# Routing and first expert of a mixture layer: expert 0 fixed as the first pass, its weights requested from the closing products on, a router held still

## The chip, the cores and the metric

One NeuronCore of a Trainium2 chip. The metric is the device time of one execution in microseconds (us), the median of three runs. One more execution was taken with the hardware profiler; all rows below come from it. PE is the matrix engine, PEld its weight load, DVE the vector engine, ACT the scalar engine, POOL GpSimd, SP the engine whose queue issues most DMAs.

## The reference

One step of a decoder of two layers for 288 tokens (256 of a prompt, 8 sequences of 4), all in float32, model width 1024. Each layer adds `W_out(sum_b sigmoid(x_n W_gate_b) * (branch_b W_branch_b))` to x, over three branches (retention, mLSTM, RWKV). Then layer 0 adds a dense SwiGLU, and layer 1 a mixture of eight experts with hidden width 1408:

```
logits = h @ router                  # h = RMSNorm(x), 288 x 8
top_v, top_i = lax.top_k(logits, 2)
probs = softmax(top_v)
y = y + combine[..., e:e+1] * ((silu(h @ wg[e]) * (h @ wu[e])) @ wd[e])    # e = 0..7
```

A final RMSNorm gives y. The experts' weights are 17.3 MB each, in float32.

## The kernel before

x, its norm xn and all weights lie with the feature on the partition, tokens along the row. Each engine's program is written out by hand and runs in order; semaphores tie them together. SP streams the weights as slabs. For the layer's branch part there is a ring of four slots (RING), of 1024 KB each; `load` waits until PE has freed the slot (slot_fr) and issues one DMA.

**Closing products** (`closing`, lines 1114 to 1141). The last eight of 24 units, 16 to 23, run in a loop of two rounds of four: PE makes the four gate products from slabs of 768 KB (L1079), waits for y_rw, and makes the four branch products (L1086), each of which frees its slab. Then eight output products from four slabs (L1139) read `mixed`; DVE adds them to X (L2074, x_mix). y_rw is written by DVE at L2039 (rw_y), in the arena, the area that also holds the later expert slabs. The norm's squares are summed on PE (L675, nm_ms), ACT takes the root, DVE the reciprocal, and then xn in eight steps (L1684).

**Routing** (`route` in PE's and DVE's program). PE makes the logits with xn as the stationary operand and the router moving: 3 tiles of 128 tokens by 8 products, 8 columns wide (L1148). It transposes xn into six half tiles (L1155), which ACT (L1607) and DVE (L2157) copy to xt. DVE picks the top two (to L2100, rt_sel). PE counts, with a triangle and a matrix of ones, how many tokens ahead chose each expert, and how many in all: 9 products (L1161, L1164, rt_pos). DVE ranks all eight experts by their counts (L2118 to L2126), writes the plan (plan_ok) and goes on to each token's place (to L2151, rt_q). `pick_tokens` turns places into a 0/1 matrix for the first pass (L2183, L2187, in_ok).

**Expert passes** (`experts`). There are eight passes, one an expert. Pass p takes the expert of rank ORDER[p] and has the fixed column count PASSES[p] = WIDTHS[ORDER[p]]: 128, 64, 96, 76, 88, 80, 64, 64. If an expert has more tokens than its width, extra passes of 64 follow, counted at run time. A pass gathers its tokens with products of xt and the 0/1 matrix (L1177 by `gather`), makes 11 gate and 11 up products from 11 slabs (L1177 again, two halves of 64 rows), and the down products in blocks of 32 tokens from six slabs (L1252). The pass after adds the result to the 288 tokens (`scatter`, L1202). The gather for pass p + 1 stands between gate/up and down of pass p. In the first pass, after f = 1, PE spreads each token's choices over the partitions (`broadcast_choices`, L1171).

**Expert slabs.** ETURNS = 17 slabs hold one expert: 0 to 3 in the ring's slots, 4 to 16 in the arena. SP waits for plan_ok, reads the expert's number, and issues all 17 (L645); for later passes each waits until PE has used the same slab of the pass before (e_used). Each slab has its own semaphore.

Every float32 product appears in the profile as two MATMUL and two LDWEIGHTS records.

## Time and profile before

| what | value |
|---|---|
| median of 3 runs | 1855.35 us (1854.37 to 1857.85) |
| the profiled execution's own time | 1862.14 us |
| its span, first to last instruction | 1860.3 us |
| mean granted clock of PE | 0.956 |
| busy: PE, PEld, DVE, ACT, POOL | 1746.0, 1378.5, 598.5, 289.4, 24.6 us |
| read from and written to memory | 275.48 MB, 10.89 MB |

Busy is summed over the whole span, and matmuls are pipelined, so 94% for PE is no measure of how near a stage is to its limit. The layer with the experts takes the last third; its stages are: closing products to 1400, norm and routing to 1439, passes to 1838, the final norm to the end.

### The profile page before, as it was taken

The page shows a single profiled execution, that of the slowest core. Times are in us where ns is not written, and L with a number is a line of the kernel's source. Part 1 is how long each engine was busy: PE and PEld are TensorE (multiplying, and loading weights), DVE is VectorE, ACT ScalarE, POOL GpSimd, SP SyncE. Part 2 cuts the span into 40 slices and gives each one's busy share as a digit, 9 for nine tenths or more (in the row PEclk, how much of TensorE's full clock was granted, in tenths as well). Part 3 has the DMA queues.
Part 4 walks back from the last instruction along what each step waited for, and adds up shares of the span by engine and source line. Part 5 has one row for each costly group of instructions (what it writes and reads, how often), then busy time and mean ns, then how long its engine had stood idle before and what let it go on. Part 6 is the DMA issues. An engine that isn't in the chain of part 4 may idle for free.

```text
span 1860.3 us, 39410 instructions
## 1 busy us (share of the span) xinstructions
PE 1746.0 (94%) x17757; PEld 1378.5 (74%) x17757; DVE 598.5 (32%) x1341; ACT 289.4 (16%) x631; POOL 24.6 (1%) x44
## 2 busy tenths in 40 slices
PE   6999999999899999999999999999997989999887
PEld 4778776788677777776677776787676978778675
DVE  3022617662511000003123526862515222212123
ACT  1321102312101000001321112221111000000001
POOL 0000000000000000000000000000000000000000
PEclk9998989999899999999998999998997999999998
DMA  7211413220253334334221412221323999889880
GB/s 287 91 68 68 158 57 126 86 75 22 58 181 113 129 109 162 121 127 197 71 88 46 177 66 97 102 59 39 101 101 147 422 385 356 331 336 366 312 345 28
DMA packets 58743, 288.80 MB, mean 155 GB/s; under 512 B 21528, under 2 KB 21976, under 8 KB 31832
## 3 DMA queue, kind: packets, MB, share of 16 engines
q1 hardware_dynamic: 39800, 266.34, 38.3%
q0 software_dynamic: 2272, 15.86, 2.2%
q10 hardware_dynamic: 16512, 4.19, 1.1%
q8 instruction: 135, 2.21, 0.5%
q14 instruction: 24, 0.20, 0.0%
HBM read 275.48 MB, written 10.89 MB: 154 GB/s over the span
## 4 chain that ended last, share of the span: by engine, by line
PE 88%; DVE 7%; issue 3%; ACT 1%; ACTq 1%; DMA 0%; DVEq 0%; SPq 0%
PE ps L1177 13%; PE ps L708 13%; PE ps L1291 9%; PE ps L1079 9%; PE ps L1252 6%; PE ps L702 5%; PE ps L1086 5%; PE ps L1300 5%; PE ps L1139 3%; PE ps L951 3%; PE ps L1202 1%; PE ps L675 1%; PE ps L806 1%; PE ps L853 1%; PE ps L781 1%
## 5 line engine op out<-in xcount | busy, mean ns | idle before, releaser
L708 PE MATMUL ps<-xn,ring 128*128 128x288 f32 x960 | 267.2, 439 | 6.5 <-DVE xn L1684 6.5
L708 PEld LDWEIGHTS ps<-xn,ring 128*128 128x128 f32 x960 | 194.9, 206 | 66.8 <-issue 10.2
L1079 PE MATMUL ps<-xn,ring 128*128 128x288 f32 x768 | 207.6, 420 | 0.0
L1079 PEld LDWEIGHTS ps<-xn,ring 128*128 128x128 f32 x768 | 146.6, 195 | 45.2 <-issue 4.6
L1291 PE MATMUL ps<-xn,ring 128*128 128x288 f32 x704 | 172.8, 409 | 3.2 <-DVE xn L1684 3.2
L1291 PEld LDWEIGHTS ps<-xn,ring 128*128 128x128 f32 x704 | 134.8, 192 | 41.1 <-issue 3.6
L1177 PE MATMUL ps<-y_ml,arena 128*64 128x64 f32 (+5 forms) x3584 | 136.5, 238 | 15.1 <-issue 14.9
L1177 PEld LDWEIGHTS ps<-y_ml,arena 128*64 128x64 f32 x3584 | 132.9, 139 | 20.3 <-issue 20.3
L1252 PE MATMUL ps<-arena,mixed 128*32 128x256 f32 x1936 | 108.8, 383 | 1.9 <-issue 1.9
L1252 PEld LDWEIGHTS ps<-arena,mixed 128*32 128x32 f32 x1936 | 62.0, 111 | 47.4 <-issue 6.3
L702 PE MATMUL ps<-ring,xn 128*128 128x256 f32 (+1 forms) x384 | 91.8, 399 | 0.0
L1300 PE MATMUL ps<-arena,ring 128*128 128x288 f32 x352 | 85.7, 406 | 0.0
L1177 PEld LDWEIGHTS ps<-y_ml,ring 128*64 128x64 f32 x2048 | 75.7, 137 | 12.5 <-issue 12.5
L1177 PE MATMUL ps<-y_ml,ring 128*64 128x64 f32 (+5 forms) x2048 | 79.1, 237 | 6.0 <-issue 5.1
L702 PEld LDWEIGHTS ps<-ring,xn 128*128 128x128 f32 (+1 forms) x384 | 64.7, 172 | 24.6 <-issue 6.6
L1300 PEld LDWEIGHTS ps<-arena,ring 128*128 128x128 f32 x352 | 66.9, 190 | 18.5
L2224 DVE TENSOR_TENSOR mixed<-ps,mixed 128x64 f32<-128x64 f32 (+5 forms) x88 | 21.4, 244 | 164.7 <-PE ps L1177 164.6
L1139 PE MATMUL ps<-mixed,ring 128*128 128x288 f32 x256 | 62.6, 407 | 2.5 <-DVE mixed L2066 2.5
L2274 DVE TENSOR_TENSOR arena<-ps,arena 128x288 f32<-128x288 f32 x22 | 10.1, 458 | 160.3 <-PE ps L1291 160.3
L1139 PEld LDWEIGHTS ps<-mixed,ring 128*128 128x128 f32 x256 | 48.5, 190 | 16.6 <-DVE mixed L2066 3.4
L1589 ACT ACTIVATE mixed<-ps 128x64 f32<-128x64 f32 (+5 forms) x88 | 21.1, 240 | 224.0 <-PE ps L1177 224.0
L1692 DVE RECIPROCAL arena<-arena 128x288 f32<-128x288 f32 x24 | 44.3, 1910 | 17.1 <-ACT arena L1430 17.1
(414 smaller groups left out, 1909.2 us busy)
## 6 DMA issues: line engine op xcount, KB each, us to landing
arena<-in_egu SPq DMA_DIRECT2D x56, 1024.0 KB, 7.2
...
```

The source lines that it names most:

```text
L702: last = mm(bank[0:m, 0:256], xn[:, k, c0:c0 + m], ring[:, s, 256 * k:256 * k + 256], start=(k == 0), stop=(k == KT - 1))
L708: last = mm(bank[:, 0:T], ring[:, s, w0:w0 + P], xn[:, k, :], start=(k == 0), stop=(k == KT - 1))
L951: last = mm(ps[half(q), out, CH * (u - 8 * g):CH * (u - 8 * g) + CH], left[half(q), u, :], right(q, u), start=True, stop=True)
L1079: last = mm(ps[:, bank, 0:T], ring[:, s, P * k:P * k + P], xn[:, k, :], start=(k == 0), stop=(k == KT - 1))
L1086: last = mm(ps[:, bank, 0:T], ring[:, s, P * (KT + k):P * (KT + k) + P], y[:, k, :], start=(k == 0), stop=(k == 3))
L1139: last = mm(ps[:, 6 + d % 2, 0:T], ring[:, s, w0:w0 + P], mixed[:, k, :], start=(k == 0), stop=(k == KT - 1))
L1177: last = mm(out(r), stationary(r), moving, start=start, stop=stop, skip_group_check=True)
L1252: last = mm(ps[TB * c:TB * c + TB, 6 + b // 2, 256 * (b % 2):256 * (b % 2) + 256], ehid[:, f, TB * b:TB * b + TB], slab_[:, w0:w0 + 256], ...
L1291: last = mm(ps[:, 2 * (f % 3) + w, 0:T], ring[:, s, w0:w0 + P], xn[:, k, :], start=(k == 0), stop=(k == KT - 1))
L1300: last = mm(ps[:, 6 + d % 2, 0:T], ring[:, s, P * f:P * f + P], hid[:, f, :], start=(f == 0), stop=(f == FT - 1))
L1692: last = dve.reciprocal(sq[:, j, :], sq[:, j, :])
L2224: TT(ehid[:, f, 0:n], ps[:, 2 * (f % 2) + 1, 0:n], esil[:, f % 3, 0:n], MUL).then_inc(e_hid.sem, 1)
```

## The change

- Expert 0 has rank 0 and is always the first pass, with 96 columns (its `tie` constant puts it above all counts). The other seven are ranked by count; their widths are 128, 96, 88, 80, 72, 64, 64. In order of the passes: 96, 72, 128, 80, 96, 88, 64, 64.
- SP's loop over the unit slabs has one round less. In layer 1 SP then waits for y_rw and the RWKV state stores, issues the plan constants and slabs 8 to 15 of expert 0, then the last four unit slabs and the output slabs, then slabs 0 to 3 as the ring's slots come free, and after the norm's sum (nm_ms) slabs 4 to 7 and 16. From pass 1 on it issues as before.
- The logits come from eight products with the router stationary and 288 columns moving, into four column groups of one bank; DVE copies the bank, and three products with the `fold` matrix add the groups and turn the result.
- Counting takes four products instead of nine.
- Expert 0's tokens are picked straight after the counts (three picks, `own`); ranking, plan and places follow. The transposes of the choices move behind f = 1 of the first pass, the broadcast behind f = 3, and `extra_passes` with them.
- ACT copies five of the six half tiles of xt and both halves of the first gathered tile. Two memsets move from DVE to POOL, behind the last x_mix.

```
-WIDTHS = (128, 96, 88, 80, 76, 64, 64, 64)
-ORDER = (0, 6, 1, 4, 2, 3, 5, 7)
+WIDTHS = (96, 128, 96, 88, 80, 72, 64, 64)
+ORDER = (0, 5, 1, 4, 2, 3, 6, 7)
...
+               ("experts", NE), ("fold", NE), ("steps", OVERS), ("extras", MAXEXTRA)):
...
+    put("tie", NE - 1 - np.arange(NE) + NE * 2 * T * (np.arange(NE) == 0))
...
+    put("fold", r[:, None] % TB == np.arange(NE)[None, :])
...
-                with sp.Fori(0, len(UNITS) // 4) as j:
+                rounds = len(UNITS) // 4 - 1
+                with sp.Fori(0, rounds) as j:
                     inner = turns.loop(j, 4)
                     for k in range(4):
                         slab = a["mix"][l, bass.ds(j * 4 + (len(EARLY) + k), 1), :, 0:12 * P]
                         load(inner, slab.rearrange("a p n -> p (a n)"), 12 * P)
-                turns.after(len(UNITS) // 4, 4)
+                turns.after(rounds, 4)
+
+                def first_expert(slabs):
+                    for k in slabs:
+                        src = a["egu"][k] if k < FT else a["edown"][k - FT, :, 0:D * len(DOWN[k - FT])]
+                        sp.dma_start(eslab(k), src).then_inc(e_ld[k].sem, 16)
+
+                if l > 0:
+                    sp.wait_ge(*rw_y(l))
+                    sp.wait_ge(st_rw.sem, 32 * (l + 1))
+                    sp.wait_ge(st_rws.sem, 32 * (l + 1))
+                    sp.dma_start(pcon, a["pcon"]).then_inc(ld_con.sem, 16)
+                    first_expert(range(FREE, ETURNS - 1))
+                for k in range(4):
+                    load(turns, a["mix"][l, len(EARLY) + 4 * rounds + k, :, 0:12 * P], 12 * P)
                 for k in range(4):
                     load(turns, a["mix"][l, len(EARLY) + len(UNITS) + k], SLOT)
...
-                sp.wait_ge(*rw_y(l))
-                sp.dma_start(pcon, a["pcon"]).then_inc(ld_con.sem, 16)
+                for _ in range(RING):
+                    s, n = turns.take()
+                    sp.wait_ge(slot_fr[s].sem, n)
+                    first_expert([s])
+                sp.wait_ge(*nm_ms(2 * l + 1))
+                first_expert([*range(RING, FREE), ETURNS - 1])
                 sp.wait_ge(*plan_ok(0))
-                for p in range(FIXED):
-                    expert(p, p == 0, sp.value_load(plan[0:1, p:p + 1], min_val=0, max_val=NE - 1))
+                for p in range(1, FIXED):
+                    expert(p, sp.value_load(plan[0:1, p:p + 1], min_val=0, max_val=NE - 1))
                 sp.wait_ge(*extra_ok(0))
                 npass = sp.value_load(plan[0:1, PLAN_N - 1:PLAN_N], min_val=1, max_val=1 + MAXEXTRA)
                 with sp.Fori(0, npass) as i:
-                    e = sp.value_load(plan[0:1, bass.ds(i + FIXED, 1)], min_val=0, max_val=NE - 1)
-                    expert(i + FIXED, False, e)
...
+                for k in range(KT):
+                    pe.wait_ge(*nm_xn(3, k + 1))
+                    c = TB * (k % 4)
+                    w0 = LW["router"] + NE * k
+                    last = mm(ps[c:c + NE, 6, 0:T], lw[:, w0:w0 + NE], xn[:, k, :], start=(k < 4), stop=(k >= 4))
+                last.then_inc(rt_part.sem, 1)
+
+                def token_tiles(first, end):
+                    for n in range(first, end):
+                        c0, m = TOK[n // 2]
+                        for k in range(4):
+                            last = pe.transpose(ps[0:m, n, P * k:P * k + P], xn[:, 4 * (n % 2) + k, c0:c0 + m],
+                                                C("ident", P))
+                        last.then_inc(xt_p.sem, 1)
+
+                token_tiles(0, 2)
+                pe.wait_ge(ld_con.sem, 64)
+                pe.wait_ge(*rt_lp(0))
                 for i, (c0, m) in enumerate(TOK):
-                    for k in range(KT):
-                        pe.wait_ge(*nm_xn(3, k + 1))
-                        last = mm(ps[0:m, 6, NE * i:NE * i + NE], xn[:, k, c0:c0 + m],
-                                  lw[:, LW["router"] + NE * k:LW["router"] + NE * k + NE],
-                                  start=(k == 0), stop=(k == KT - 1))
+                    last = mm(ps[0:m, 7, NE * i:NE * i + NE], gate[:, 0, c0:c0 + m], PCON("fold", NE), start=True,
+                              stop=True)
                 last.then_inc(rt_lg.sem, 1)
-                for n in range(6):
-                    c0, m = TOK[n // 2]
-                    for k in range(4):
-                        last = pe.transpose(ps[0:m, n, P * k:P * k + P], xn[:, 4 * (n % 2) + k, c0:c0 + m], C("ident", P))
-                    last.then_inc(xt_p.sem, 1)
-                pe.wait_ge(ld_con.sem, 64)
+                token_tiles(2, 6)
                 pe.wait_ge(*rt_sel(0))
-                for i in range(3):
-                    for k in range(i + 1):
-                        mm(ps[:, 7, NE * i:NE * i + NE], PCON("tri", P) if k == i else C("ones", P), gt[:, k, :],
-                           start=(k == 0), stop=(k == i))
-                for k in range(3):
-                    last = mm(ps[:, 7, 32:32 + NE], C("ones", P), gt[:, k, :], start=(k == 0), stop=(k == 2))
+                mm(ps[:, 7, 64:88], PCON("tri", P), gt, start=True, stop=False, skip_group_check=True)
+                for n in range(3):
+                    last = mm(ps[:, 7, 72 + NE * n:96], C("ones", P), gt[:, 0:3 - n, :], start=False, stop=(n == 2),
+                              skip_group_check=True)
                 last.then_inc(rt_pos.sem, 1)
+
+            def choices():
+
+                pe.wait_ge(*rt_q(0))
+                for i, (c0, m) in enumerate(TOK):
+                    last = pe.transpose(ps[0:4, 6, c0:c0 + m], q[0:m, :, i], C("ident", m, m))
+                last.then_inc(rt_ct.sem, 1)
...
                         if first:
-                            broadcast_choices()
+                            choices()
                         else:
                             scatter(p - 1, blocks, 0)
+                    if f == 3 and first:
+                        broadcast_choices()
                     if f == 3 and not first:
                         scatter(p - 1, blocks, 1)
...
-                pe.wait_ge(xt_a.sem, 3)
-                pe.wait_ge(xt_d.sem, 3)
+                pe.wait_ge(xt_a.sem, 5)
+                pe.wait_ge(xt_d.sem, 1)
                 gather(0, PASSES[0])
-                pe.wait_ge(*rt_q(0))
-                for i, (c0, m) in enumerate(TOK):
-                    last = pe.transpose(ps[0:4, 6, c0:c0 + m], q[0:m, :, i], C("ident", m, m))
-                last.then_inc(rt_ct.sem, 1)
...
-                    if f == 1 and first:
+                    if f == 3 and first:
                         for v, bank in ((0, 7), (2, 5)):
                             act.wait_ge(rt_bc.sem, v + 1)
                             A(chosen[:, v, :], ps[:, bank, 0:T], ACT.Copy).then_inc(rt_cha.sem, 1)
...
-                act.wait_ge(*rt_e(0))
-                A(ex, ex, ACT.Exp).then_inc(rt_ex.sem, 1)
-                for n in (0, 2, 4):
+                for n in range(5):
+                    if n == 4:
+                        act.wait_ge(*rt_e(0))
+                        A(ex, ex, ACT.Exp).then_inc(rt_ex.sem, 1)
+                        act.wait_ge(*rt_sel(0))
                     act.wait_ge(xt_p.sem, n + 1)
                     m = TOK[n // 2][1]
-                    if n == 4:
-                        act.wait_ge(*rt_sel(0))
-                    A(xt[0:m, n // 2, 0:512], ps[0:m, n, :], ACT.Copy).then_inc(xt_a.sem, 1)
+                    h = 512 * (n % 2)
+                    A(xt[0:m, n // 2, h:h + 512], ps[0:m, n, :], ACT.Copy).then_inc(xt_a.sem, 1)
                 gathered(0, PASSES[0])
+                act.wait_ge(ga_p.sem, 2)
+                A(xg[:, 4:8, 0:PASSES[0]], ps[:, 5, :].rearrange("p (k n) -> p k n", k=4)[:, :, 0:PASSES[0]], ACT.Copy)\
+                    .then_inc(ga_d.sem, 1)
...
-                dve.memset(yg, 0.0)
                 link(dve.memset(lg, 0.0))
-                dve.memset(xt[:, 2, :], 0.0)
+                dve.wait_ge(*rt_part(0))
+                dve.tensor_copy(gate[:, 0, :], ps[:, 6, 0:T]).then_inc(rt_lp.sem, 1)
                 dve.wait_ge(*rt_lg(0))
-                dve.tensor_copy(lg[:, 0:2, :], ps[:, 6, 0:16].rearrange("p (i e) -> p i e", i=2))
-                link(dve.tensor_copy(lg[0:TS, 2, :], ps[0:TS, 6, 16:24]))
+                dve.tensor_copy(lg[:, 0:2, :], ps[:, 7, 0:16].rearrange("p (i e) -> p i e", i=2))
+                link(dve.tensor_copy(lg[0:TS, 2, :], ps[0:TS, 7, 16:24]))
...
+                dve.wait_ge(*rt_zero(0))
                 dve.sem_inc(rt_sel.sem, 1)
+                dve.wait_ge(xt_p.sem, 6)
+                dve.tensor_copy(xt[0:TS, 2, 512:D], ps[0:TS, 5, :]).then_inc(xt_d.sem, 1)
+
+                dve.wait_ge(*rt_pos(0))
+                dve.tensor_copy(cnt, ps[:, 7, 88:96])
+                link(dve.tensor_copy(pos, ps[:, 7, 64:88].rearrange("p (i e) -> p i e", i=3)))
+                link(STT(own, pos[:, :, 0], 1.0, gt[:, :, 0], ADD, MUL))
+                for i in range(3):
+                    last = TSC(pick_in[:, i, 0:PASSES[0]], PCON("iota", PASSES[0]), own[:, i:i + 1], None, ALU.is_equal)
+                last.then_inc(in_ok.sem, 1)
...
-                dve.wait_ge(*rt_pos(0))
-                link(dve.tensor_copy(cnt, ps[:, 7, 32:32 + NE]))
-                dve.tensor_copy(pos, ps[:, 7, 0:24].rearrange("p (i e) -> p i e", i=3))
...
-                pick_tokens(0, PASSES[0])
-                for n in (1, 3, 5):
-                    dve.wait_ge(xt_p.sem, n + 1)
-                    m = TOK[n // 2][1]
-                    dve.tensor_copy(xt[0:m, n // 2, 512:D], ps[0:m, n, :]).then_inc(xt_d.sem, 1)
...
-                dve.wait_ge(*rt_ct(0))
-                dve.tensor_copy(gate_rows[0:4, 0, :], ps[0:4, 6, 0:T]).then_inc(rt_cr.sem, 1)
-                next_places(0)
...
-                    if f == 1:
+                    if f == 1 and not first:
+                        scattered(p - 1, 0)
+                    if f == 2:
                         if first:
-                            for v, bank in ((1, 4), (3, 6)):
-                                dve.wait_ge(rt_bc.sem, v + 1)
-                                dve.tensor_copy(chosen[:, v, :], ps[:, bank, 0:T]).then_inc(rt_chd.sem, 1)
-                        else:
-                            scattered(p - 1, 0)
-                    if f == 2:
+                            dve.wait_ge(*rt_ct(0))
+                            dve.tensor_copy(gate_rows[0:4, 0, :], ps[0:4, 6, 0:T]).then_inc(rt_cr.sem, 1)
+                            next_places(0)
                         pick_tokens(p + 1, after)
                         next_places(p + 1)
+                    if f == 3 and first:
+                        extra_passes()
+                        for v, bank in ((1, 4), (3, 6)):
+                            dve.wait_ge(rt_bc.sem, v + 1)
+                            dve.tensor_copy(chosen[:, v, :], ps[:, bank, 0:T]).then_inc(rt_chd.sem, 1)
...
-                gathered(0, PASSES[0])
-                extra_passes()
...
+            pool.wait_ge(*x_mix(DEPTH - 1, 8))
+            pool.memset(yg, 0.0)
+            pool.memset(xt[:, 2, :], 0.0).then_inc(rt_zero.sem, 1)
...
```

## Rows read from the trace of the kernel before

**Rows 1.** Windows, pass by pass: start:end length, busy PE PEld DVE ACT POOL, clock, DMA, GB/s
```profile
1439.14:1501.93 62.79, 62.79 (x1161) 54.03 (x1161) 12.19 (x40) 4.26 (x14) 0.00 (x0) 1.00 1.01 422
1501.93:1549.90 47.97, 40.36 (x1045) 33.95 (x1041) 10.75 (x34) 3.55 (x13) 0.00 (x0) 1.00 0.91 346
1549.90:1603.58 53.68, 50.82 (x1100) 42.40 (x1096) 11.42 (x35) 3.78 (x13) 0.00 (x0) 1.00 0.92 354
1603.58:1654.40 50.82, 46.43 (x1113) 37.97 (x1112) 11.72 (x36) 3.64 (x13) 0.00 (x0) 1.00 0.88 340
1654.40:1703.39 48.99, 48.47 (x1114) 41.09 (x1112) 11.78 (x36) 3.73 (x13) 0.00 (x0) 1.00 0.94 360
1703.39:1757.98 54.59, 48.16 (x1117) 38.68 (x1113) 11.64 (x36) 3.60 (x13) 0.00 (x0) 0.97 0.84 321
1757.98:1802.69 44.71, 39.51 (x1029) 33.53 (x1025) 10.30 (x34) 4.04 (x14) 0.00 (x0) 0.96 0.97 371
```

**Rows 2.** PE timeline in two passes, and the instruction queue between 1500 and 1550 us
```profile
1455.45 24.62 PE L1177 MATMUL ps<-y_ml,arena 128*64 128x128 f32 x448
...
1482.80 19.20 PE L1252 MATMUL ps<-arena,mixed 128*32 128x256 f32 x352
...
1722.57 4.64 PE L1177 MATMUL ps<-y_ml,arena 128*64 128x80 f32 x127 [1.65 <-issue]
1728.86 4.64 PE L1177 MATMUL ps<-y_ml,arena 128*64 128x80 f32 x127 [1.65 <-issue]
...
q8 instruction: 9, 0.15, 1.1%
```

**Rows 3.** Routing: two rows of the timeline, then the chain of waits
```profile
1406.52 3.52 DVE L1684 SCALAR_TENSOR_TENSOR xn<-X,vec,rstd 128x288 f32<-128x288 f32 x8
...
1417.54 0.18 DVE L2100 TENSOR_TENSOR arena<-arena 128x24 f32<-128x24 f32 x1
...
1407.10 7.96 PE ps L1148 x48
1415.06 3.98 PE ps L1155 x24
1419.04 1.24 PE ps L1161 x12
...
1420.99 0.18 DVE arena L2118
...
1427.77 0.69 DVE mixed L2183 x3
...
1429.37 1.79 DVE con L2157 x3
...
1431.25 7.06 PE ps L1177 x96
```

**Rows 4.** Timeline of the closing products, SP, DVE and PE
```profile
1310.42 57.48 SPq L601 DMA_DIRECT2D ring<-in_mix  x9
...
1329.61 1.36 DVE L2039 TENSOR_TENSOR arena<-arena 128x1152 f32<-128x1152 f32 x1
...
1344.09 15.68 PE L1079 MATMUL ps<-xn,ring 128*128 128x288 f32 x64
```

**Rows 5.** Landing times of L645 (1420:1470) and L601 (1300:1400); one window; SP's issues
```profile
DMA to landing us min/median/max: 4.8/21.8/27.7
...
DMA to landing us min/median/max: 4.1/5.7/7.9
...
1420.00:1430.00 10.00, 0.95 (x9) 0.86 (x8) 7.88 (x41) 0.00 (x0) 0.00 (x0) 0.72 0.50 187
...
1423.96 2.16 SPq L645 DMA_DIRECT2D ring<-in_egu  x4
```

**Rows 6.** PE's busy time and granted clock in two stretches after a pause
```profile
1315.00:1322.00 7.00, 6.29 (x13) 0.51 0.55 130
...
1431.00:1434.00 3.00, 2.75 (x26) 0.50 1.03 434
```

36 lines of the change are left out of this document (18 added, 18 removed).

## The prediction

> **What bounds the kernel now.** I read the windows by stage first, because the engine shares are averages over stages. From 1439.14 us on, eight passes over eight experts follow each other, 62.79 us for the first, 44 to 55 us for the next six [rows 1], and one more of two blocks, which the change leaves as it is. The matrix engine (PE) is busy in most of each window, but the DMA share stands beside it at 0.84 to 1.01, so two limits compete there. The gap list settles which. In the 80-column pass PE runs 127 matmul records, pauses 1.65 us, runs 127 records, pauses again [rows 2]. A slab holds 64 records of this work (704 over 11 slabs), so two slabs would be 128, and these pauses do not sit on slab borders. 127 matmuls with their weight loads are 254 instructions, and the instruction queue brings packets one every 50/9 = 5.6 us [rows 2]. I read the pauses as waits for instructions that arrive slowly beside full data queues. The expert weights are ahead of PE: the first slab is requested at 1423.96 [rows 5] and wanted at 1439.14, and one slab takes 2.5 us to move where PE works 3.5 on it (64 records of 0.055). So the passes are set by PE work or by about 6 us per 127 records, whichever is longer.
>
> Ahead of the passes lies the routing, a chain of small steps from 1407.10 to 1439.14 in which PE mostly waits or runs at half clock [rows 3]. Ahead of that are the closing products, where PE has no pause: from 1344.09 it takes the second four gate slabs right behind the first four's branch products [rows 4].
>
> **Part 1: expert 0 is loaded during the closing products.** No wait for expert weights is removed by that, since PE does not wait for them now. What counts is what the new transfers stand in front of. SP issues everything on one queue. Now the last four unit slabs are requested as their slots come free (the nine issues from 1310.42 on [rows 4]). After the change SP first waits for y_rw, which DVE finishes at 1329.61 + 1.36 = 1330.97 [rows 4], then issues the plan constants and slabs 8 to 15, eight of 1024 KB, and only then unit slab 20. The waits for the state stores are over by then. The queue serves in order: the slab loads issued between 1420 and 1470 needed 21.8 us to land in the median, against 5.7 for the unit and output slabs with a nearly free queue [rows 5], with 422 GB/s moved [rows 1]. Start of transfer: 1.87 MB were moved between 1420 and 1430 (187 GB/s) [rows 5], 4.4 us at 422 GB/s, so the first byte flowed at 1425.6, some 1.6 us after the first issue at 1423.96, which is what plan_ok releases [rows 5]. Hence: 1331.0 + 1.6 + 0.4 (the plan constants, some 150 KB) + 8 x 1.049 MB at 422 GB/s (8 x 2.49 = 19.9) = 1352.9, then 0.786 MB of unit slab 20 (1.9) and its landing (0.6, what the shortest time of 4.1 us [rows 5] leaves after 1.6 and 1.9): 1355.4. PE wants the slab at about 1344.2. It stands still for 11.2 us. The next three slabs land 1.9 us apart, faster than the 3.9 us per slab that PE needs (15.68/4 [rows 4]), so nothing is added there. After such a pause the granted clock is at 0.5 (1.2 of 2.4 GHz) and stays there for a while after work resumes: 0.51 over the 7 us from 1315 and 0.50 over the 3 us from 1431 [rows 6]. Half of 3 to 6.5 us is lost: 1.5 to 3.2, I take 2. **Part 1: +13.2 us** (9.5 if the queue starts sooner and the clock holds, 14.5 above).
>
> The remaining nine slabs cost nothing: four go as the output slabs are freed, five (4.7 MB, 11 us) from the norm's sum on, and the first is wanted 20 us later. That cover is the routing; if it shrank under 11 us slab 4 would be late first.
>
> **Part 2: routing.** Times here are on the old clock, without part 1's shift. xn comes in eight steps of 0.44 until 1410.04 [rows 3]. The old router ran 48 records of 8 columns after that, until 1415.06. The new one keeps the router still and moves 288 columns in eight products, in four column groups, and only the last follows xn: 1.0 us at half clock, 1411.0. The copy to SBUF (0.5, as one step of xn over the same 288 columns) lies beside eight transposes (3.98/24 x 8 = 1.3), to 1412.4; three folding products (6 records like the router's, 0.166 each) to 1413.4. That is 1.7 us earlier than 1415.06. The selection is unchanged, 1415.06 to 1417.72 [rows 3], so 1416.1. The POOL memsets that take the place of DVE's run since x_mix, long done. Old: counting waits for the transposes until 1419.04, and DVE has its 18 records at 1420.99. New: 8 records (0.10 each [rows 3], or 0.16 at half clock), 1417.1. Then DVE: cnt, pos, own at 0.2 each, three picks of 96 columns (0.69 x 96/128 = 0.5), gather may start at 1418.4. Old start: 1431.25, because the whole ranking (1420.99 to 1427.77), six picks and three copies (1.79) lay before it [rows 3]. The copies go to ACT, five at 0.6 and one table load, over by 1417.3. The ranking moves behind in_ok: plan at about 1422, choices at 1427. It delays SP's plan_ok, but SP first needs e_used at 1427 anyway; PE's choices come after two slabs, at 1430. The gather is 96 records with 96 instead of 128 columns: 7.06 x 3/4 = 5.3, evacuation by ACT 0.7 (0.83 now, 1438.31 to 1439.14): PE starts the first pass at 1424.4 where it started at 1439.14, 14.7 earlier. The three transposes of the choices move from before into the first pass (+0.5). The added DVE work at f = 2 and 3 (about 2.6 and 3 us) stays within the slab it has in hand. **Part 2: -14.2 us** (-17 if the busier router brings the clock back early, -11.5 if the gather runs at half clock throughout, 8.2 us).
>
> **Part 3: widths.** Passes were 128, 64, 96, 76, 88, 80, 64, 64 columns; they become 96, 72, 128, 80, 96, 88, 64, 64. Equivalently a 76 and a 64 are exchanged for a 96 and a 72, one block of 32 tokens more. Priced as PE work: a record costs 24.62/448 = 0.0550 us at 128 columns and 4.64/127 = 0.0365 at 80 [rows 2], 0.000385 per column. 28 columns x 800 records = 8.6; one block more is 88 down records at 19.20/352 = 0.0545 [rows 2], 4.8, and 16 scatter records, 1.0. Sum 14.4, the upper end. Priced by the windows, where the instruction pauses swallow part: out go 50.82 and the mean of the two-block passes 47.97 and 44.71, together 97.2; in come 53.68 and, for 72, 50.82 again, 104.5 [rows 1]. **Part 3: +7.3 us.** Lower end 2.3, if a pass of 96 goes like the one of 88 (48.99 plus 2.5 of columns) and 72 takes 48. I take the windows, since they contain both limits.
>
> The Trainium skill, page Runtime: NRT & Kernel Launch, section Instruction fetch mechanics, says that PE's instruction memory holds 2048 instructions, refilled in blocks of 256, and that crossing a block is mostly hidden. The spacing of the pauses agrees with the block, their length does not agree with hidden. By that page the full 14.4 would be due, and the sum 13.4.
>
> **Sum:** 13.2 - 14.2 + 7.3 = +6.3 us. The profiled execution took 1862.14 us (span 1860.3) and the median of the three runs is 1855.35; the difference is carried over: 1861.7. A measurement of this kernel can tell about 0.2%, 3.7 us, from no change.
>
> **Rivals.** (a) Unit slab 20 is not late, the faster side: the eight transfers do not hold it back, or end before 1344. Then parts 2 and 3 remain, -6.9: 1848.5. It decides below a stall of about 5 us, that is if the slab lands before 1349. For it: the closing stage moves little data now. Against it: one queue, landing times of 21.8 us behind others [rows 5]. 0.18. (b) The instruction pauses hide most of the width, part 3 is 2.3: 13.2 - 14.2 + 2.3 = +1.3, 1856.7. For it: 96 columns cost 53.68 and 80 columns 54.59 [rows 1]. 0.22. (c) The width is paid in full and the clock stays low in the gather: 13.2 - 11.5 + 14.4 = +16.1, 1871.5. 0.10. (d) Expert 0, now fixed to 96 columns, gets more tokens and needs an extra pass of two blocks, about +45 (44.71 [rows 1]). The reference's own router on its inputs gives the experts 48, 74, 43, 115, 66, 88, 62, 80 tokens; 48 fits into 96, and ranked 115, 88, 80, 74, 66, 62, 43 fit the widths. 0.02. The forecast has 0.48.
>
> **The numbers.** Range 1847.5 to 1870: down to (a), up to just under (c); about 2 in 10 outside. Faster by over 3.7: (a) and the low edge of the others, 0.20. Within: most of (b) and the lower part of the forecast, 0.26. Slower: 0.54.
>
> **What would show it.** In the changed profile: an idle stretch of 9 to 12 us ahead of the second gate products, ended by a DMA, with the DMA share near 1 from 1332 to 1353; logits 1.7 us earlier against xn and the gather about 13 us earlier; the first pass starting 14 to 15 us nearer to the norm's end; passes summing to 5 to 10 us more, still with pauses every 127 records. The prediction is wrong if PE has no pause in the closing products, if the passes together grow by under 2 or over 14 us, or if the first pass waits for its slabs.

## Result and profile after

The changed kernel took 1863.57 us in the median of 20 runs, the kernel before 1858.90 on the same chip: a ratio of 1.0026, 95% interval 1.0014 to 1.0039, or +4.7 us (+2.6 to +7.2). The prediction said 1861.7, +6.3 against its base of 1855.35; that base was a median of three runs and lies 3.5 below the median of twenty, so what can be compared is the difference. Its profiled execution took 1863.47 us (span 1861.3), the one of before 1862.14 (span 1860.3); the spans differ by 1.0 only because the start of the closing products varies between executions (1336.33 before, 1330.28 after, 1338.51 in a second profile of the same changed kernel). So I compare stages from there on. First the four stages of the changed kernel. Columns: busy time and records of PE, PEld, DVE, ACT, POOL, then PE's granted clock, DMA share, GB/s.

```profile
1330.28:1380.50 50.22, 34.34 (x130) 25.87 (x128) 7.33 (x16) 3.34 (x6) 0.00 (x0) 0.83 0.67 269
1380.50:1436.40 55.90, 49.95 (x294) 38.09 (x295) 19.21 (x78) 10.54 (x20) 1.84 (x2) 0.94 0.52 198
1436.40:1841.71 405.31, 387.19 (x8675) 328.28 (x8675) 92.90 (x295) 30.75 (x105) 0.00 (x0) 0.98 0.80 302
1841.71:1861.34 19.63, 6.60 (x49) 4.39 (x48) 8.57 (x17) 5.45 (x11) 0.00 (x0) 0.80 0.15 61
```

The same four stages of the kernel before:

```profile
1336.33:1368.77 32.44, 31.21 (x130) 24.14 (x128) 7.33 (x16) 3.34 (x6) 0.00 (x0) 1.00 0.45 162
1368.77:1439.14 70.37, 56.54 (x333) 47.87 (x334) 24.81 (x94) 10.39 (x17) 0.00 (x0) 0.85 0.28 114
1439.14:1837.57 398.43, 370.11 (x8568) 309.77 (x8568) 89.15 (x283) 29.08 (x104) 0.00 (x0) 0.99 0.86 336
1837.57:1860.29 22.72, 9.69 (x48) 6.22 (x48) 8.57 (x17) 5.45 (x11) 0.00 (x0) 0.72 0.13 53
```

| stage | before | after | change | after, second profile |
|---|---|---|---|---|
| first four branch products to output products | 32.44 | 50.22 | +17.8 | +16.2 |
| output products, norm, routing, first gather | 70.37 | 55.90 | -14.5 | -15.1 |
| expert passes | 398.43 | 405.31 | +6.9 | +4.9 |
| end | 22.72 | 19.63 | -3.1 | 0.0 |
| sum | 523.96 | 531.06 | +7.1 | +6.0 |

The end stage belongs to no part of the change: in before PE was busy for 9.69 us there at clock 0.72, in after for 6.60 at 0.80, with the same work (48 and 49 records in the window), and the second profile of the changed kernel shows 22.72 again.

**The new wait.** Timeline of the closing products after the change. It answers to [rows 4]; the bracket gives PE's idle time and what ended it.

```profile
1314.76 15.68 PE L1104 MATMUL ps<-xn,ring 128*128 128x288 f32 x64
...
1326.62 1.36 DVE L2081 TENSOR_TENSOR arena<-arena 128x1152 f32<-128x1152 f32 x1
...
1328.00 0.34 SPq L643 DMA_DIRECT2D arena<-in_pcon  x1
1328.39 1.37 SPq L637 DMA_DIRECT2D arena<-in_egu  x3
1329.81 2.99 SPq L637 DMA_DIRECT2D arena<-in_edown  x5
...
1330.28 7.92 PE L1111 MATMUL ps<-arena,ring 128*128 128x288 f32 x32
...
1332.85 46.78 SPq L609 DMA_DIRECT2D ring<-in_mix  x8
...
1352.86 18.65 PE L1104 MATMUL ps<-xn,ring 128*128 128x288 f32 x64 [14.65 <-DMA ring<-in_mix]
```

The chain can be read off line by line. DVE ends y_rw at 1327.98; SP issues the plan constants and the eight expert slabs at once; only at 1332.85 does it request unit slab 20; PE ends its branch products at 1338.2 and stands still until that slab has landed. Windows of the same stretch show what the queue and the clock did:

```profile
1330.00:1340.00 10.00, 8.20 (x34) 6.08 (x32) 3.67 (x8) 0.41 (x1) 0.00 (x0) 1.00 0.97 405
1340.00:1350.00 10.00, 0.00 (x0) 0.00 (x0) 0.00 (x0) 0.00 (x0) 0.00 (x0) 0.58 1.01 426
...
1353.00:1356.00 3.00, 3.00 (x7) 2.14 (x8) 0.00 (x0) 0.00 (x0) 0.00 (x0) 0.50 1.01 389
1356.00:1360.00 4.00, 4.00 (x13) 2.92 (x12) 0.00 (x0) 0.04 (x1) 0.00 (x0) 0.66 0.41 171
1360.00:1370.00 10.00, 10.00 (x43) 7.85 (x42) 0.00 (x0) 2.48 (x4) 0.00 (x0) 1.00 0.00 0
```

From 1340 to 1350 the DMA engines were busy throughout (share 1.01, 426 GB/s), and PE did nothing at all meanwhile. PE resumes at 0.50, that is 1.2 GHz, and has 2.4 GHz back after about 6 us; the 64 records take 18.65 us instead of 15.68. In the second profile of the changed kernel the pause is 14.20 us and the records take 17.55.

**The routing.** Its steps after the change, answering to [rows 3]:

```profile
1418.83 4.13 PE L1174 MATMUL ps<-xn,lw 128*8 128x288 f32 x16 [3.13 <-DVE xn L1726]
...
1427.59 0.40 PE L1194 MATMUL ps<-arena 128*128 128x24 f32 x2 [0.90 <-DVEq L2144]
...
1429.94 5.83 PE L1217 MATMUL ps<-mixed,con 128*64 128x96 f32 x96 [1.30 <-DVE mixed L2153]
...
1436.40 5.50 PE L1217 MATMUL ps<-y_ml,ring 128*64 128x96 f32 x128 [0.63 <-issue]
```

The first router product comes as soon as xn is there, after 3.13 us in which PE waited for it, the counting 8.8 us behind it, the gather 11.1 us behind it. The first pass follows the gather after 6.46 us, and its row waits for no slab ("issue", 0.63).

**The passes**, one window each, answering to [rows 1]. In order the widths are 96, 72, 128, 80, 96, 88, 64 and 64 columns.

```profile
1436.40:1487.50 51.10, 51.10 (x1076) 43.88 (x1076) 12.15 (x47) 5.20 (x15) 0.00 (x0) 0.97 0.79 305
1487.50:1537.76 50.26, 47.80 (x1116) 40.12 (x1113) 12.02 (x36) 3.74 (x13) 0.00 (x0) 0.97 0.91 347
1537.76:1602.42 64.66, 64.66 (x1204) 55.37 (x1200) 13.40 (x38) 4.09 (x13) 0.00 (x0) 1.00 0.77 276
1602.42:1656.17 53.75, 49.88 (x1132) 41.97 (x1128) 12.10 (x36) 3.70 (x13) 0.00 (x0) 0.97 0.85 317
1656.17:1707.02 50.85, 50.85 (x1116) 43.53 (x1112) 11.95 (x36) 3.83 (x13) 0.00 (x0) 1.00 0.90 344
1707.02:1759.13 52.11, 49.06 (x1117) 40.59 (x1113) 11.65 (x36) 3.67 (x13) 0.00 (x0) 1.00 0.87 335
1759.13:1804.76 45.63, 38.28 (x1026) 33.02 (x1025) 10.21 (x34) 4.05 (x14) 0.00 (x0) 1.00 0.97 369
1804.76:1841.71 36.95, 35.56 (x912) 29.79 (x912) 9.42 (x32) 2.47 (x11) 0.00 (x0) 0.95 0.17 69
```

In this execution the passes of 96 and 128 columns have PE busy in the whole window; all idle time lies in the narrower ones. The 80-column pass takes 2.90 us longer than the 96-column one after it, although PE has 0.97 us less work in it.

### The profile page after: what moved, and what is told of

Same layout as the page of the kernel before. It is cut to its first block, busy times and chain, and to the rows that moved or that the text cites. A ratio compares the mean times of both kernels' runs of the same rounds, so it can differ in the third digit from the quotient of the medians.

```text
span 1861.3 us, 39486 instructions
## 1 busy us (share of the span) xinstructions
PE 1749.9 (94%) x17825; PEld 1382.7 (74%) x17825; DVE 596.6 (32%) x1338; ACT 291.0 (16%) x634; POOL 26.4 (1%) x46
## 3 DMA queue, kind: packets, MB, share of 16 engines
q8 instruction: 135, 2.21, 0.5%
## 4 chain that ended last, share of the span: by engine, by line
PE 87%; DVE 7%; issue 2%; DMA 2%; ACT 1%; ACTq 1%; SPq 0%; DVEq 0%
PE ps L1217 14%; PE ps L733 12%; PE ps L1329 9%; PE ps L1104 8%; PE ps L1294 6%; PE ps L727 5%; PE ps L1338 5%; PE ps L1111 4%; PE ps L1164 3%; PE ps L976 3%; PE ps L1242 1%; DVE arena L1734 1%; PE ps L700 1%; DMA ring<-in_mix 1%; PE ps L831 1%
## 5 line engine op out<-in xcount | busy, mean ns | idle before, releaser
L733 PEld LDWEIGHTS ps<-xn,ring 128*128 128x128 f32 x960 | 194.7, 206 | 66.7 <-issue 10.2
L1104 PE MATMUL ps<-xn,ring 128*128 128x288 f32 x768 | 208.1, 420 | 14.7 <-DMA ring<-in_mix 14.7
L1217 PE MATMUL ps<-y_ml,arena 128*64 128x96 f32 (+5 forms) x3584 | 142.7, 243 | 11.6 <-issue 11.5
L1217 PEld LDWEIGHTS ps<-y_ml,arena 128*64 128x64 f32 x3584 | 139.7, 140 | 16.2 <-issue 16.1
L1294 PEld LDWEIGHTS ps<-arena,mixed 128*32 128x32 f32 x2024 | 65.8, 110 | 45.6 <-issue 3.6
L727 PEld LDWEIGHTS ps<-ring,xn 128*128 128x128 f32 (+1 forms) x384 | 64.7, 172 | 24.4 <-issue 6.4
L2260 DVE TENSOR_TENSOR mixed<-ps,mixed 128x96 f32<-128x96 f32 (+5 forms) x88 | 21.7, 247 | 156.8 <-PE ps L1217 156.7
L1627 ACT ACTIVATE mixed<-ps 128x96 f32<-128x96 f32 (+5 forms) x88 | 21.4, 243 | 227.7 <-PE ps L1217 227.7
```

What stands on the lines that cost most here:

```text
L727: last = mm(bank[0:m, 0:256], xn[:, k, c0:c0 + m], ring[:, s, 256 * k:256 * k + 256], start=(k == 0), stop=(k == KT - 1))
L733: last = mm(bank[:, 0:T], ring[:, s, w0:w0 + P], xn[:, k, :], start=(k == 0), stop=(k == KT - 1))
L1104: last = mm(ps[:, bank, 0:T], ring[:, s, P * k:P * k + P], xn[:, k, :], start=(k == 0), stop=(k == KT - 1))
L1217: last = mm(out(r), stationary(r), moving, start=start, stop=stop, skip_group_check=True)
L1294: last = mm(ps[TB * c:TB * c + TB, 6 + b // 2, 256 * (b % 2):256 * (b % 2) + 256], ehid[:, f, TB * b:TB * b + TB], slab_[:, w0:w0 + 256], ...
L2260: TT(ehid[:, f, 0:n], ps[:, 2 * (f % 2) + 1, 0:n], esil[:, f % 3, 0:n], MUL).then_inc(e_hid.sem, 1)
```

## Experiments

My theory was the prediction's: the eight expert slabs hold back unit slab 20 and cost 11 to 16 us, the routing gives some 14, the widths cost 5 to 7. The main rival: the closing stage would lose its time anyway, and fetching expert 0 early earns something in the passes that pays for it. Each kernel ran against the kernel before on its own chip (medians of before: 1860.84, 1859.96, 1864.29 and 1860.90 in the four sets).

**The unit slabs first.** The eight expert slabs stay early, but behind everything that the closing products need.

```diff
                     sp.dma_start(pcon, a["pcon"]).then_inc(ld_con.sem, 16)
-                    first_expert(range(FREE, ETURNS - 1))
                 for k in range(4):
                     load(turns, a["mix"][l, len(EARLY) + 4 * rounds + k, :, 0:12 * P], 12 * P)
...
+                first_expert(range(FREE, ETURNS - 1))
                 for _ in range(RING):
```

> The changed kernel with one move: slabs 8 to 15 of expert 0 are issued behind the last unit and output slabs, no longer in front of them. Queue theory (the eight transfers stand ahead of unit slab 20 in SP's queue): PE's pause of 14.65 us in the closing products is gone, and with it 1.5 to 3 us at half clock, so the stretch from the end of the first branch products to the first pass falls from 98.2 to about 80.5 us, and the time from about 6 us above the kernel before to 10 to 13 us below it, ratio 0.993 to 0.995. Rival 1 (the pause comes from the transfers' own load on memory, wherever they stand): the pause moves into the output products, and the time falls by under 5 us. Rival 2 (slabs requested so late that the first pass waits for them): the pause moves to the first pass, one over 2 us there.

Measured: 1849.71 us, ratio 0.9930 (0.9898 to 0.9962). The kernel was run again with more rounds beside the changed one:

> The changed kernel itself, beside its variants on one chip. Both theories: ratio 1.001 to 1.004 to the kernel before, with a pause of 11 to 15 us ahead of the second gate products.

> units_first once more, in more rounds. Queue theory: 14.65 us of pause and up to 3 us of low clock are gone, so 15 to 18 us under changed_again, ratio 0.991 to 0.995. Rival (part of the pause comes back elsewhere): under 12 us below changed_again.

Measured: changed 1863.87, ratio 1.0027 (1.0000 to 1.0054); units first 1849.03, ratio 0.9940 (0.9917 to 0.9964). Between the two ratios lie 0.0087, or 16.2 us; between the two medians 14.8. Stages of the kernel with the unit slabs first:

```profile
1338.84:1371.27 32.43, 31.20 (x129) 24.13 (x127) 7.33 (x16) 3.34 (x6) 0.00 (x0) 1.00 0.46 167
1371.27:1424.77 53.50, 47.54 (x295) 36.14 (x295) 17.78 (x68) 10.55 (x20) 1.84 (x2) 1.00 0.88 360
1424.77:1827.29 402.52, 385.12 (x8675) 326.06 (x8675) 94.36 (x305) 30.74 (x105) 0.00 (x0) 0.99 0.81 304
```

The closing stage is at 32.43 us again, the time of before, and its clock at 1.00. So the order of eight DMAs was the whole of the +17.8, and nothing else in the change costs time there. The pause did not move to the output products or to the first pass either, which were the two rivals put on record.

**Four of the eight in front.**

```diff
-                    first_expert(range(FREE, ETURNS - 1))
+                    first_expert(range(FREE, FREE + 4))
...
+                first_expert(range(FREE + 4, ETURNS - 1))
                 for _ in range(RING):
```

> The changed kernel with four slabs (8 to 11) in front of unit slab 20 instead of eight, the other four behind the output slabs. Queue theory: the pause before the second gate products falls by 4 x 2.49 = 9.9, from 14.65 to 4 to 6 us, depending on how late the first branch products end, with 1 to 3 us of low clock behind it; ratio 0.996 to 0.999, 3 to 7 us above units_first. Rival (any transfer in front costs a fixed delay, such as a change of queue state or address tables): the pause stays above 10 us.

Measured: 1856.38 us, ratio 0.9986 (0.9950 to 1.0022). Its closing stage:

```profile
1331.07:1341.86 10.79, 7.92 (x33) 5.90 (x32) 3.67 (x8) 0.41 (x1) 0.00 (x0) 1.00 1.01 419
1341.86:1366.64 24.78, 23.55 (x97) 18.18 (x97) 3.66 (x8) 2.92 (x5) 0.00 (x0) 1.00 0.45 168
```

PE is idle for 10.79 - 7.92 = 2.87 us before the second gate products, and the clock holds. Four slabs fewer are 4 x 2.49 = 10.0 us of the queue, and the idle time fell by 14.65 - 2.87 = 11.8; the excess is that PE came to its branch products 1.7 us later in this execution, 3.97 us after the issue of the plan constants (1331.07 - 1327.10) where it had been 2.28. The dose and the stall go together, although the pause is shorter than the 4 to 6 us expected, and the low clock expected behind it did not come. The interval of the ratio is too wide for more.

**Everything after the norm's sum**, so that expert 0 is fixed but not fetched early at all.

```diff
-                    first_expert(range(FREE, ETURNS - 1))
...
-                    first_expert([s])
                 sp.wait_ge(*nm_ms(2 * l + 1))
-                first_expert([*range(RING, FREE), ETURNS - 1])
+                first_expert(range(ETURNS))
```

> The changed kernel, but all 17 slabs of expert 0 are issued behind the norm's sum, none during the closing products. Queue theory: fixing expert 0 frees the load from the plan, and nothing more is needed: 17 slabs at 2.49 us each land from about 12 us before the first pass starts, one per 2.5 us, and PE uses one per 2.75 us in the gate products, so the time is that of units_first within 2 us, ratio 0.993 to 0.996. Rival (the early start during the closing products earns something): slower than units_first by more than 4 us, with a pause in the first pass. A second rival, slower instruction fetch beside full queues in the first pass of 96 columns: pauses of 1 to 2 us each 127 records there, 3 to 5 us in all.

> all_after_norm once more. Its trace has no wait for a slab, but the first two passes take 52.8 and 53.0 us against 51.1 and 50.2 for units_first, with instruction pauses of 0.6 to 1.9 us, since the queue of slab loads is still full then. Queue theory with slow instruction fetch: 3 to 5 us above units_first, ratio 0.994 to 0.998. Rival 1 (the place of the loads does not matter once nothing stands in front of the units): within 1.5 us of units_first. Rival 2 (the 11 us between the first medians were real): more than 8 us above units_first.

Measured: 1858.79 us, ratio 0.9989 (0.9959 to 1.0019), then with more rounds 1852.03, ratio 0.9962 (0.9939 to 0.9985). Beside units_first_again that is 0.0022 slower, some 4 us, though the two intervals overlap. The first two passes of this kernel:

```profile
1422.95:1476.50 53.55, 51.68 (x1076) 44.13 (x1076) 12.35 (x48) 5.18 (x15) 0.00 (x0) 0.97 1.01 422
1476.50:1530.28 53.78, 46.89 (x1117) 38.70 (x1113) 12.10 (x36) 3.73 (x13) 0.00 (x0) 1.00 0.93 375
```

and of the one with the unit slabs first:

```profile
1424.76:1475.85 51.09, 51.09 (x1075) 43.88 (x1075) 12.32 (x48) 5.20 (x15) 0.00 (x0) 0.97 0.80 306
1475.85:1526.88 51.03, 46.19 (x1116) 38.44 (x1112) 12.03 (x36) 3.73 (x13) 0.00 (x0) 1.00 0.90 343
```

In these two profiles early fetching earns 2.46 and 2.75 us, but not because slabs came late: no wait of PE in this trace ends with a DMA. The DMA queue is full in the first pass (1.01, 422 GB/s) where it was at 0.80, and PE's pauses stand in it.

**The choice of tokens late.** From the kernel with the unit slabs first, the three picks of expert 0 and in_ok are moved behind the whole ranking:

```diff
-                for i in range(3):
-                    last = TSC(pick_in[:, i, 0:PASSES[0]], PCON("iota", PASSES[0]), own[:, i:i + 1], None, ALU.is_equal)
-                last.then_inc(in_ok.sem, 1)
...
                 dve.sem_inc(rt_q.sem, 1)
+                for i in range(3):
+                    last = TSC(pick_in[:, i, 0:PASSES[0]], PCON("iota", PASSES[0]), own[:, i:i + 1], None, ALU.is_equal)
+                last.then_inc(in_ok.sem, 1)
```

> units_first, but the three picks that release the gather stand behind the whole ranking and the places (behind rt_q) instead of in front. Theory (the gain in the routing comes from fixing expert 0, whose tokens are picked straight after the counts): DVE's chain from the picks to rt_q, 1429.71 to 1438.01 in the changed kernel, moves in front of the gather, +8.3 us, plus 0 to 3 us of low clock in a gather that starts after a longer idle stretch; the stretch from the output products to the first pass grows from 53.5 to 62 to 65 us, ratio to the kernel before 0.997 to 1.000. Rival (the gain comes from the router products and the four counting products, and the ranking is hidden beside slabs and transposes): grows by under 3 us.

Measured: 1856.66 us, ratio 0.9990 (0.9971 to 1.0009), 0.0050 or 9.3 us above units_first_again. From output products to first pass it took 63.75 us, against 53.50 and 55.14 in the two profiles of units first: +9.4 to their mean. PE's row of the gather reads:

```profile
1417.99 6.01 PE L1217 MATMUL ps<-mixed,con 128*64 128x96 f32 x96 [9.72 <-DVE mixed L2200]
```

The gather begins 10.78 us after the counting (1417.99 - 1407.21) where it began 2.36 us after it (1419.96 - 1417.60): 8.4 us of the 9.4 are DVE's chain, the rest is the clock in the gather (6.01 us for its records against 4.18 and 5.66). So fixing the first expert is worth 8 to 9 us of the routing's gain: its tokens need no ranking.

**The old products.** From the same kernel, the 24 logit products with xn stationary and nine counting products are put back; the early choice stays.

```diff
-                for k in range(KT):
-                    pe.wait_ge(*nm_xn(3, k + 1))
...
-                    last = mm(ps[c:c + NE, 6, 0:T], lw[:, w0:w0 + NE], xn[:, k, :], start=(k < 4), stop=(k >= 4))
+                for i, (c0, m) in enumerate(TOK):
...
+                    for k in range(KT):
+                        pe.wait_ge(*nm_xn(3, k + 1))
...
+                        last = mm(ps[0:m, 7, NE * i:NE * i + NE], xn[:, k, c0:c0 + m], lw[:, w0:w0 + NE],
+                                  start=(k == 0), stop=(k == KT - 1))
...
-                mm(ps[:, 7, 64:88], PCON("tri", P), gt, start=True, stop=False, skip_group_check=True)
-                for n in range(3):
-                    last = mm(ps[:, 7, 72 + NE * n:96], C("ones", P), gt[:, 0:3 - n, :], start=False, stop=(n == 2),
...
+                for i in range(3):
+                    for k in range(i + 1):
+                        mm(ps[:, 7, 64 + NE * i:72 + NE * i], PCON("tri", P) if k == i else C("ones", P), gt[:, k, :],
...
+                for k in range(3):
+                    last = mm(ps[:, 7, 88:96], C("ones", P), gt[:, k, :], start=(k == 0), stop=(k == 2))
```

> units_first with the old forms of both small products: 24 logit products with xn stationary, and nine counting products; the picks stay early. Sum's theory: logits 1.7 us later (plus the clock: the 8-column products ran at 0.5 from 1407 to 1417 in the kernel before, while 288-column products let it rise sooner, 0 to 2 us) and counts 1.1 us later, since 18 records take 0.10 each and not 8; the stretch from the output products to the first pass grows by 2.5 to 5 us, to 56.5 to 60, ratio to the kernel before 0.995 to 0.997. Rival (the transposes and copies set the pace, and the form of the products is covered): grows by under 1 us.

Measured: 1857.57 us, ratio 0.9969 (0.9937 to 1.0000), which overlaps with units_first_again. The stage says more: 61.63 us against 53.50 and 55.14, +7.3 to their mean, and I had expected 2.5 to 5. Its PE timeline:

```profile
1410.77 8.14 PE L1176 MATMUL ps<-lw,xn 128*128 128x8 f32 x48 [3.13 <-DVE xn L1728]
1418.84 5.38 PE L1186 MATMUL ps<-con,xn 128*128 128x128 f32 x24
...
1424.01 0.43 PE L1196 MATMUL ps<-arena 128*128 128x8 f32 x2
...
1427.60 5.83 PE L1219 MATMUL ps<-mixed,con 128*64 128x96 f32 x96 [1.30 <-DVE mixed L2155]
```

and the same steps with the new products:

```profile
1409.61 3.66 PE L1174 MATMUL ps<-xn,lw 128*8 128x288 f32 x16 [3.13 <-DVE xn L1726]
...
1417.60 0.40 PE L1194 MATMUL ps<-arena 128*128 128x24 f32 x2 [0.90 <-DVEq L2144]
...
1419.96 4.18 PE L1217 MATMUL ps<-mixed,con 128*64 128x96 f32 x96 [1.30 <-DVE mixed L2153]
```

Counting starts 13.2 us after the first router product in the one and 8.0 in the other. The old logits take 8.14 us, and the 24 transposes stand behind them at 0.22 each, ahead of the counting. In the new order eight of them run beside DVE's copy and sixteen while DVE selects. A second part is the clock: over this stage it was 0.86 with the old products and 1.00 with the new, and the gather takes 5.83 instead of 4.18. The clock enters the 5.2 us between the two countings as well: the kernel before, with the same old products, ran its transposes in 4.05 us and began counting 11.8 us after the first router product. How much of that clock belongs to the products is not settled, since with the new ones the changed kernel and the second profile of units first had 0.94, with gathers of 5.83 and 5.66.

**The widths alone**, from the kernel before:

```diff
-WIDTHS = (128, 96, 88, 80, 76, 64, 64, 64)
-ORDER = (0, 6, 1, 4, 2, 3, 5, 7)
+WIDTHS = (128, 96, 96, 88, 80, 72, 64, 64)
+ORDER = (0, 5, 1, 4, 2, 3, 6, 7)
```

> The kernel before with the new multiset of widths alone: 128, 96, 96, 88, 80, 72, 64, 64 by rank, passes of 128, 72, 96, 80, 96, 88, 64, 64 columns, one block of 32 tokens more. Forecast theory (part of the added PE work is covered by instruction pauses): +7.3 us over the kernel before, ratio 1.003 to 1.005. Rival full price: +14.4 us, ratio 1.0065 to 1.0085, with the pauses of the passes as long as before, 28 us. Rival covered: +2.3 us, ratio 1.000 to 1.002, pauses under 18 us.

Measured: 1870.55 us, ratio 1.0054 (1.0024 to 1.0084), +10.0 us; its profile puts only 4.8 into the passes and 2.4 into the stage ahead of them, which the edit does not touch:

```profile
1373.19:1445.91 72.72, 58.89 (x334) 49.89 (x334) 24.81 (x94) 10.38 (x17) 0.00 (x0) 0.81 0.29 115
1445.91:1849.18 403.27, 382.15 (x8672) 324.37 (x8672) 91.02 (x286) 29.33 (x104) 0.00 (x0) 0.99 0.86 331
```

PE has 382.15 - 370.11 = 12.0 us more work, and its idle time falls from 28.3 to 21.1. Part of the price is paid out of the pauses. The interval (+4.5 to +15.6 us) excludes the rival of +2.3; it doesn't exclude the full 14.4, but that rival named pauses as long as before, and they are 7.2 shorter.

**What the pauses are.** If they are late slabs or late instructions, both depend on the traffic of slabs, so I cut that to a quarter and left PE's instructions as they are. This kernel leaves out three quarters of each slab from the second expert on, so the sums of seven experts are not the reference's.

```diff
+                        src = src[:, :, 0:width // 4]
-                        sp.dma_start(eslab(k)[:, 0:width], src.rearrange("a p n -> p (a n)")).then_inc(e_ld[k].sem, 16)
+                        sp.dma_start(eslab(k)[:, 0:width // 4], src.rearrange("a p n -> p (a n)")).then_inc(e_ld[k].sem, 16)
```

> units_first, but each slab load of the second to the last expert moves a quarter of its columns (the rest of the slab keeps expert 0's weights, so the sums of seven experts are others; PE's work is the same). Fetch theory (the pauses every 127 records are instruction packets held up beside slab loads): the pauses of the passes, 17.2 to 17.4 us, fall under 5 us and the passes from 402.5 to about 386 to 390 us; ratio to the kernel before 0.984 to 0.988. Rival (PE's own supply of instructions cannot keep up at these widths, whatever the data queues carry): pauses of 14 us or more remain, passes above 398.

Measured: 1825.05 us, ratio 0.9797 (0.9739 to 0.9855). Its passes:

```profile
1420.21:1798.95 378.74, 377.54 (x8675) 320.88 (x8675) 94.19 (x305) 30.74 (x105) 0.00 (x0) 1.00 0.26 83
```

PE is idle for 1.2 us in 379, where it was for 17.4 in 403. The rest is 7.6 us less busy time for the same records, which I did not expect (386 to 390 us were forecast for the passes) and cannot account for. To tell late slabs from late instructions I set PE's pauses beside the landing of instruction packets. First the timeline of PE in the 80-column pass of the changed kernel, which answers to [rows 2]:

```profile
1621.76 4.64 PE L1217 MATMUL ps<-y_ml,arena 128*64 128x80 f32 x127 [1.09 <-issue]
1627.23 4.64 PE L1217 MATMUL ps<-y_ml,arena 128*64 128x80 f32 x127 [0.83 <-issue]
```

and then, worked out from the trace's DMA records, how long before PE resumed the last packet of the instruction queue had landed:

```
PE resumes   pause   packet landed before it
1621.76      1.09    1.45
1627.23      0.83    1.28
1633.82      1.94    1.27
```

In the passes of the changed kernel 15 of 16 pauses over 0.35 us end 1.1 to 1.6 us after such a landing, in the kernel before 22 of 24, although such moments make up only a tenth of the passes' time. There are 69 such packets of 16 KB for the 17350 records of PE and PEld in the passes, one per 251, and each takes 0.95 us in the median whether the slabs flow or not, so what varies is when they are served. The pauses are waits for instructions.

**A narrower first pass.** Again from the kernel with the unit slabs first. Expert 0 gets 48 tokens, and 64 columns hold them. With the extra passes they would hold up to 256 tokens, so this kernel leaves out the cover for inputs that send more of the 288 to expert 0:

```diff
-WIDTHS = (96, 128, 96, 88, 80, 72, 64, 64)
+WIDTHS = (64, 128, 96, 88, 80, 72, 64, 64)
```

> units_first with a first pass of 64 columns instead of 96 (two blocks of 32 tokens instead of three; expert 0 has 48 tokens). Full price, as in the prediction's upper end: 800 records x 32 columns x 0.000385 = 9.9, one block of down and scatter 5.8, together 15.7 us less, ratio to units_first 0.9915. Window theory (instruction fetch puts a floor of 5 to 6 us under every 127 records): the block's 5.8 in full and of the 9.9 about a third to a half, since pauses appear that the 96 columns covered: 9 to 11 us less, ratio to the kernel before 0.988 to 0.990. Covered price: under 6 us less.

Measured: 1842.11 us, ratio 0.9893 (0.9852 to 0.9935), against 0.9940 (0.9917 to 0.9964) for units first in another set. All its passes, and the first alone:

```profile
1419.73:1820.88 401.15, 372.76 (x8571) 315.75 (x8571) 93.52 (x307) 30.45 (x105) 0.00 (x0) 0.99 0.81 305
...
1419.73:1467.30 47.57, 40.47 (x988) 33.14 (x988) 13.17 (x60) 4.90 (x15) 0.00 (x0) 0.93 0.79 295
```

The pass that was narrowed shows it best. It has 51.09 - 40.47 = 10.6 us less PE work than with the unit slabs first, and it is 3.5 us shorter: 7.1 us of pauses stand where there were none. Over all passes 12.4 us of work are gone, the time is 1.4 us less and the idle time rose from 17.4 to 28.4; the difference to 3.5 lies in passes that the edit does not touch. This is the strongest case of width being paid out of the pauses. The gather gives another 1.2 us (3.02 instead of 4.18), so the profile does not show the 9 to 11 us that I expected. The ratio does lie where I put it (0.988 to 0.990), 0.0047 or some 9 us under units first, but the two intervals overlap, so whether the time fell by more than the profile says is open.

**Halved loads.** From the second expert on, each slab comes as two DMAs of half the bytes. The idea was that another queue's packet would have more places to get in:

```diff
-                        sp.dma_start(eslab(k)[:, 0:width], src.rearrange("a p n -> p (a n)")).then_inc(e_ld[k].sem, 16)
+                        for h in (0, width // 2):
+                            part = src[:, :, h:h + width // 2].rearrange("a p n -> p (a n)")
+                            sp.dma_start(eslab(k)[:, h:h + width // 2], part).then_inc(e_ld[k].sem, 16)
...
-                pe.wait_ge(e_ld[k].sem, p * 16 + 16)
+                pe.wait_ge(e_ld[k].sem, p * 32 + 16)
```

> units_first, but from the second expert on each slab is loaded by two DMAs of half its columns (4 KB rows instead of 8 KB), the same bytes in all. quarter_slabs has shown that the pauses go with the data beside the instruction packets; this asks whether the size of the pieces matters or the bytes. Piece theory (an instruction packet waits for pieces of slab data under way on its DMA engine, so halved pieces halve the wait): pauses fall from 17.3 to 5 to 10 us and the passes from 402.5 to 392 to 398, ratio to the kernel before 0.988 to 0.992. Byte theory (it waits for the queue's bytes, however cut): pauses 14 to 21 us, passes 399 to 407, ratio 0.992 to 0.996. A third, more issues and smaller rows slow the transfer itself: PE waits for slabs, passes above 410.

Measured: 1857.60 us, ratio 0.9980 (0.9952 to 1.0007). The passes took 412.57 us, with 26.4 us of PE idle in place of 17.4, and no wait of PE ended with a slab. Smaller pieces did not help, which refutes the theory that they halve the wait. That they harm is not shown: the kernel with the old products, whose slabs come whole, took 411.50 us with 24.7 of idle, and the interval overlaps with that of units_first_again.

## Why the prediction was right, and where it was off

The sign, the size and the three parts came out as forecast: +6.3 was said, +4.7 (+2.6 to +7.2) measured, and the stages of the two profiles of the changed kernel give +7.1 and +6.0. That the sum comes so near is partly luck: part 1 cost 4.6 and 3.0 us more than forecast, and what made up for it was the end stage in the first profile (-3.1, no part of the change) and part 3 in the second (-2.4).

**Part 1, said +13.2, measured +17.8 and +16.2.** The mechanism is shown, by the row that names the DMA and by the kernel with the unit slabs first. The transfer side of the step held: unit slab 20 was said to land 24.4 us after y_rw, and PE resumed 24.9 us after it (1352.86 - 1327.98), in the second profile 24.4. What was mis-sized is the time at which PE wants the slab. I took it from the profile of before, 13.2 us after y_rw. There PE came to its branch products 5.4 us after y_rw, in both profiles of the changed kernel 2.3 us. The 3.1 us between the two are clock. In before, the row ahead of the gate products (L723) took 4.21 us, at a granted clock of 0.50, and the four gate products 16.79:

```profile
1315.71 4.21 PE L723 MATMUL ps<-arena,con 128*128 128x288 f32 x8 [2.90 <-ACT arena L1427]
```

In the changed kernel the same row took 2.21 us, at 1.00, and the gate products 15.68:

```profile
1312.71 2.21 PE L748 MATMUL ps<-arena,con 128*128 128x288 f32 x8 [2.87 <-ACT arena L1465]
```

y_rw itself did not move with that: it ended 15.3 us after the start of this row in both. Over the 14 profiles of this case PE came 2.3 us after y_rw in seven, 4.0 us in six, and 5.4 us in the one that I had read. In the changed kernel PE was ready 10.2 us after y_rw, and the pause was 14.65 instead of 11.2. A stall is a difference of two times, and I had checked only one of them for scatter. The low clock after it cost 18.65 - 15.68 = 2.97 instead of 2 (1.87 in the second profile), within the 1.5 to 3.2 that I gave.

**Part 2, said -14.7 to the start of the first pass, measured -14.5 and -15.1.** The ledger of the routing held step by step, counted from the first router product: the counts were said to reach DVE after 10.0 us and did after 9.85 (13.9 in before), the gather after 11.3 and 11.1, the first pass after 17.3 and 17.6. (The terms before the gather add up to 1418.2, not 1418.4.) Of the gain, 8 to 9 us are the early choice of tokens, which is what fixing expert 0 buys. The products were forecast at 3.9 us to the counts, and 4.0 is what before and changed kernel show. Putting them back in the kernel with the unit slabs first cost 7.3, more than that, partly by a lower clock. The two experiments together explain more than the gain (9.4 + 7.3 = 16.7), so they overlap or include scatter of the clock; the gather itself ran at 5.83 us in the changed kernel where I had taken 5.3, and at 4.18 with the clock at 1.00.

**Part 3, said +7.3, measured +6.9, +4.9, and +4.8 for the widths alone.** It lies in my range of 2.3 to 14.4, and the reason was right: PE's busy time grows by 17.1 us in the changed kernel and by 12.0 with the widths alone, and the instruction pauses give some back. That the first figure is so near is luck. The exchange that I priced, a 96 and a 72 for a 76 and a 64, cost 51.10 + 50.26 - 50.82 - 47.97 = 2.6; the other 4.3 came from passes of unchanged width, where the 88-column pass grew by 3.1 and the 96-column one shrank by 2.8. Passes of equal width differ by 2 to 3 us by where the pauses fall, so a price by windows cannot be better than that. PE's pauses fell from 28.3 to 18.1 us.

The Trainium skill, page Runtime: NRT & Kernel Launch, section Instruction fetch mechanics, would have the crossing of an instruction block mostly hidden. Here 16.2 us of 403 were not, and came back when the slabs' bytes were quartered, where 1.2 us of 379 agree with it; the runs decide against the sentence for this kernel with its DMA share at 0.8 to 0.9.

**The rivals.** (a), slab 20 not late, is refuted in the changed kernel and realised by the experiment: it was said to give -6.9, and units first gave -11.2 (1859.96 x 0.0060; the interval reaches from -6.7 to -15.4). (b), pauses hide all of the width, came true in part. (c) and (d) did not happen: the first pass has no extra block.

What was said to show it did show: an idle stretch ended by a DMA (14.65 us where 9 to 12 were named), the DMA share near 1 until the slab landed, the gather 13.0 us nearer to the first router product (24.15 - 11.11), the logits 2.0 us earlier against xn, passes summing to 6.9 and 4.9 us more where 5 to 10 were named, the first pass without a wait for its slabs.

**Left open.** The passes of kernels with nearly the same code took 402.4 to 411.5 us (units first 402.5 and 402.4, old products 411.5, pick late 409.1). PE's idle time explains 5 to 7 us of it, and how the code falls on the 256-instruction blocks may be behind them, which was not tried.
